# The softmax heads' product of probabilities and first values in three rounded products, in a two-block transformer forward on one Trainium2 core

## The reference

```python
s = jnp.einsum('bhid,bhjd->bhij', q, k) * scale     # 256 x 256 for each head
s = jnp.where(mask, s, -jnp.inf)
p = jax.nn.softmax(s, axis=-1)
o = jnp.einsum('bhij,bhjd->bhid', p, v)             # the product that is changed
```

## Time and profile before

| what | value |
|---|---|
| time of the profiled execution | 1799.72 us |
| its span | 1797.8 us |
| PE busy | 1788.5 us, 99% |
| DVE busy | 1243.6 us, 69% |
| ACT busy | 1037.5 us, 58% |
| POOL busy | 154.5 us, 9% |
| median of the timed runs | 1800.09 us |

### The profile page before, as it was taken

The page is one execution under the profiler, slowest core; times in us unless marked ns, Lnnn a source line. Parts: engine busy times, 40 slices in busy tenths (PEclk is TensorE's granted clock), DMA queues, the critical chain, the costliest instruction groups (busy, mean ns, idle before and its releaser), DMA issues.

```text
span 1797.8 us, 27226 instructions
## 1 busy us (share of the span) xinstructions
PE 1788.5 (99%) x10842; PEld 1622.1 (90%) x10842; DVE 1243.6 (69%) x1711; ACT 1037.5 (58%) x1638; POOL 154.5 (9%) x116
## 2 busy tenths in 40 slices
PE   9999999999999999999999999999999999999998
PEld 8999889888899999998889999898888999989987
DVE  6665656665666897687658888776565888767764
ACT  7435546774557765875554345576454444457853
POOL 0000000110011111100001211000000111100110
PEclk9999999999999999999999999999999999999999
DMA  9557555555555555445566655555555655555564
GB/s 370 200 171 225 182 182 190 181 175 195 190 189 167 171 171 175 154 165 169 194 207 202 199 188 176 193 180 172 190 193 196 201 199 181 174 192 183 168 220 140
DMA packets 95901, 340.30 MB, mean 189 GB/s; under 512 B 10800, under 2 KB 11184, under 8 KB 95648
## 3 DMA queue, kind: packets, MB, share of 16 engines
q1 hardware_dynamic: 94400, 334.44, 55.9%
q0 software_dynamic: 944, 3.61, 0.6%
q10 hardware_dynamic: 432, 0.53, 0.1%
HBM read 336.44 MB, written 2.10 MB: 188 GB/s over the span
## 4 chain that ended last, share of the span: by engine, by line
PE 99%; DMA 0%; DVE 0%; issue 0%; ACT 0%; DVEq 0%
PE ACC L838 15%; PE ACC L840 15%; PE ACC L839 15%; PE ACC L846 12%; PE ACC L843 12%; PE ACC L845 6%; PE ACC L844 6%; PE ACC L851 2%; PE ACC L852 2%; PE ACC L853 2%; PE PM L961 1%; PE PM L998 1%; PE PM L976 1%; PE PM L890 1%; PE PM L960 0%; PE PM L999 0%
## 5 line engine op out<-in xcount | busy, mean ns | idle before, releaser
L1654 DVE TENSOR_TENSOR WL<-RAW,WH 128x1024 fp32r<-128x1024 f32 (+2 forms) x631 | 793.4, 1272 | 421.8 <-ACT WH L1222 420.3
L1222 ACT ACTIVATE WH<-RAW 128x1024 fp32r<-128x1024 f32 (+2 forms) x632 | 646.9, 1038 | 382.5 <-PE ACC L840 190.2
L843 PE MATMUL ACC<-XHL,WH 128*128 128x512 f32 x1024 | 395.6, 386 | 0.0
L846 PE MATMUL ACC<-XHL,WH 128*128 128x512 f32 x1024 | 391.2, 382 | 0.0
L838 PE MATMUL ACC<-WH,XHL 128*128 128x512 f32 (+1 forms) x788 | 296.5, 376 | 0.0
L840 PE MATMUL ACC<-WH,XHL 128*128 128x512 f32 (+1 forms) x788 | 291.9, 370 | 0.0
L839 PE MATMUL ACC<-WL,XHL 128*128 128x512 f32 (+1 forms) x788 | 291.9, 370 | 0.0
L845 PE MATMUL ACC<-XHL,WL 128*128 128x256 f32 x1024 | 281.6, 275 | 0.0
L844 PE MATMUL ACC<-XHL,WL 128*128 128x256 f32 x1024 | 279.1, 273 | 0.0
L845 PEld LDWEIGHTS ACC<-XHL,WL 128*128 128x128 f32 x1024 | 193.5, 189 | 27.4
L844 PEld LDWEIGHTS ACC<-XHL,WL 128*128 128x128 f32 x1024 | 193.6, 189 | 26.5
(11 more groups left out here) (406 smaller groups left out, 2344.0 us busy)
## 6 DMA issues: line engine op xcount, KB each, us to landing
RAW<-in_w SPq DMA_DIRECT2D x607, 512.0 KB, 3.3
RAW<-in_wv SPq DMA_DIRECT2D x24, 344.0 KB, 3.2
X<-in_x SPq DMA_DIRECT2D x4, 512.0 KB, 11.9
Y<-in_xT SPq DMA_DIRECT2D x3, 512.0 KB, 10.6
out<-Y SPq DMA_DIRECT2D x6, 256.0 KB, 3.6
S<-in_bias POOLq DMA_DIRECT2D x8, 128.0 KB, 2.3
S<-in_od_gate_w POOLq DMA_DIRECT2D x1, 1024.0 KB, 7.1
S<-in_final_norm POOLq DMA_DIRECT2D x1, 1024.0 KB, 6.3
```

The costliest lines, as they stand in the source:

```text
L843: e.matmul(acc[0], wh0, pairs, start=f, stop=False, skip_group_check=True)
L846: m = e.matmul(acc[1], wh1, pairs, start=False, stop=l, skip_group_check=True)
L1222: e.activation(hi, src, ACT.Copy).then_inc(s_hi)
L1654: e.tensor_tensor(lo, src, hi.bitcast(F32), ALU.subtract).then_inc(s_lo)
```

## The change

For the 32 softmax heads with values of 128 features ("narrow"), the product with the first 128 keys is made of three products of rounded parts, as the projections are. `vh` and `vl` are the high part and the remainder of the head's first values; `PH` and `PL` are those of the first 256 columns of the turned probabilities. The product with the second 128 keys stays plain.

- ACT, step `value_split`, three slots before `pT` (seven before `pv`): copies the 128 columns of first values, rounded, to one of two slots. POOL, in the same slot: subtracts for the remainder.
- ACT, step `pT`: in place of one copy of 384 columns, one of the last 128 and one of the first 256, rounded, into the single buffer PH.
- DVE, new step `pl`, two slots after `pT` and two before `pv`: subtracts PH from the bank in PSUM for the remainder PL. The bank is held until then.
- PE, step `pv`: waits for `s_vl` and `s_pl`, then three fp32r products of 256 columns and the plain one as before.
- The new buffers lie where ZC lies, which only layer 1 uses.

```diff
-        ZC = sb("ZC", 1024)
+        with ExitStack() as first:
+            ZC = sb("ZC", 1024, F32, first)
+        PVH = sb("PVH", 1024, F32R)
...
+        PH, PL = PVH[:, 0:256], PVH[:, 256:512]
+        def value_slot(g):
+            at = 512 + 256 * (g % 2)
+            return PVH[:, at:at + 128], PVH[:, at + 128:at + 256]
...
                         put(slot + every * r + late, step, first + h + (4 if step[0] == "p" else 0), 1)
+                        if step == "pT":
+                            put(slot + every * r + late - 3, "value_split", first + h + 4)
+                            put(slot + every * r + late + 2, "pl", first + h + 4)
...
@@ tensor, pT @@
-                read_out[b] = (s_pts, TURN[g])
+                read_out[b] = (s_pl, nth_narrow(g)) if narrow(g) else (s_pts, TURN[g])
...
@@ tensor, pv @@
-                    e.matmul(o[:, 0:256], v[0], p[:, 0:256], start=True, stop=False, skip_group_check=True)
+                    vh, vl = value_slot(g)
+                    e.wait_ge(s_vl, nth_narrow(g))
+                    e.wait_ge(s_pl, nth_narrow(g))
+                    e.matmul(o[:, 0:256], vh, PH, start=True, stop=False, skip_group_check=True)
+                    e.matmul(o[:, 0:256], vl, PH, start=False, stop=False, skip_group_check=True)
+                    e.matmul(o[:, 0:256], vh, PL, start=False, stop=False, skip_group_check=True)
                     e.matmul(o[:, 128:256], v[1], p[:, 256:384], start=False, stop=True, skip_group_check=True).then_inc(s_pv)
...
@@ scalar @@
                 e.wait_ge(s_pt, TURN[g])
-                e.activation(pt_slot(g), PM[b][:, 0:384], ACT.Copy).then_inc(s_pts)
+                if not narrow(g):
+                    e.activation(pt_slot(g), PM[b][:, 0:384], ACT.Copy).then_inc(s_pts)
+                    return
+                if g > 4:
+                    e.wait_ge(s_pv, TURN[g] - 1)
+                e.activation(pt_slot(g)[:, 256:384], PM[b][:, 256:384], ACT.Copy).then_inc(s_pts)
+                e.activation(PH, PM[b][:, 0:256], ACT.Copy).then_inc(s_ph)
+            def value_split(g, _):
+                v, job = values_at(g)
+                n = nth_narrow(g)
+                e.wait_ge(s_evA, at_A(*job))
+                if n > 2:
+                    e.wait_ge(s_pv, TURN[g] - 2)
+                e.activation(value_slot(g)[0], v[0], ACT.Copy).then_inc(s_vh)
...
@@ vector @@
+            def probabilities_low(g, _):
+                b = PT_BANK[g]
+                e.wait_ge(s_ph, nth_narrow(g))
+                e.tensor_tensor(PL, PM[b][:, 0:256], PH.bitcast(F32), ALU.subtract).then_inc(s_pl)
...
@@ gpsimd @@
+            def value_split(g, _):
+                v, _ = values_at(g)
+                vh, vl = value_slot(g)
+                e.wait_ge(s_vh, nth_narrow(g))
+                e.tensor_tensor(vl, v[0], vh.bitcast(F32), ALU.subtract).then_inc(s_vl)
```

More of the change, by code:

```diff
@@ L409, in program, with values_at, narrow, nth_narrow @@
         TURN = list(accumulate(0 if g >= 4 and first_of_pair(g - 4) else 1 for g in range(44)))
+        def values_at(g):
+            layer, n, h = head_of(g - 4)
+            c = slice(128 * h, 128 * h + 128)
+            return [tok(3 * n + 2 if layer else 5)[:, t, c] for t in range(2)], (layer, f"v{n}" if layer else "va", h // 4)
+        def narrow(g):
+            return g >= 4 and not is_diff(g - 4)
+        def nth_narrow(g):
+            return g - 3 if g < 12 else g - 11
         def masked(a):
@@ L613, in program @@
                     FEW_BANK = got[0]
+        PT_BANK = {item: got for x in plan.values() for step, item, got in x if step == "pT"}
         def around(p):
@@ L647, in program @@
             sem(n) for n in ("s_dg", "s_pa", "s_pe", "s_pk", "s_pc", "s_pm", "s_zero", "s_am", "s_tri", "s_la"))
-        s_neg = sem("s_neg")
+        s_neg, s_ph, s_pl, s_vh, s_vl = (sem(n) for n in ("s_neg", "s_ph", "s_pl", "s_vh", "s_vl"))
         s_lx, s_lc, s_ly, s_ld, s_so, s_sd, s_sa, s_or, s_on, s_gd1 = (
@@ L987, in values_of @@
                     return [tok(2)[:, t, c] for t in range(2)], 256, (2, "v0", h // 4)
-                c = slice(128 * h, 128 * h + 128)
-                return [tok(3 * n + 2 if layer else 5)[:, t, c] for t in range(2)], 128, (layer, f"v{n}" if layer else "va", h // 4)
+                v, job = values_at(g)
+                return v, 128, job
             def pv(g, b):
@@ L1594, in scalar @@
             steps = {"seed": seed, "warm": warm, "xt": xt, "squares": squares, "root": root, "rms_a": rms_a, "gates1": gates1, "selectors": selectors, "decay_cols": decay_cols,
-                     "decay_rows": decay_rows, "cols": columns_step, "rows": rows, "decay": decay, "pT": pT,
+                     "decay_rows": decay_rows, "cols": columns_step, "rows": rows, "decay": decay, "pT": pT, "value_split": value_split,
                      "norm_qk": norm_qk, "qkT": qkT, "scores": scores, "normal": normal, "silu_z": silu_z, "yT": yT, "mix1": mix1, "pv": pv, "ty": ty, "copied": copied, "silu": silu, "decays1": decays1,
@@ L2136, in vector @@
                      "decay": decay, "mscores": mscores, "norm_qk": norm_qk, "scale_k": scale_k, "scores": scores, "mix1": mix1,
-                     "mix2": mix2, "rsum": rsum, "pv": pv,
+                     "mix2": mix2, "rsum": rsum, "pl": probabilities_low, "pv": pv,
                      "yT": yT, "ty": ty, "taps": taps,
@@ L2286, in gained @@
                     e.tensor_tensor(Y3[:, t, c], X3[:, t, c], S0[:, c], ALU.mult).then_inc(s_gn)
-            steps = {"norm_qk": norm_qk, "scale_k": scale_k, "scores": scores, "gate_z": gate_z, "cols": columns_step, "tri": tri, "gate_w": gate_w,
+            steps = {"norm_qk": norm_qk, "scale_k": scale_k, "scores": scores, "value_split": value_split, "gate_z": gate_z, "cols": columns_step, "tri": tri, "gate_w": gate_w,
                      "gate_lru": gate_lru, "gate_c": gate_c, "load_mask": load_mask, "load_gain": load_gain, "gained": gained}
```

## The result

| | median us | lowest to highest | runs |
|---|---|---|---|
| before | 1800.13 | 1799.44 to 1802.01 | 10 |
| changed | 1805.47 | 1803.59 to 1806.86 | 10 |

The changed kernel is slower: the ratio is 1.0025, with a 95% interval from 1.0017 to 1.0033. Its profiled execution took 1803.84 us (span 1801.9), 4.1 us more than that of before.

A forecast was written before the change was run, and what follows sets the result against it. PE, busy 99% of the span, was taken as the bound. Lateness 6.8 plus 0.5 less gain 2.5 gave +4.8 us on the profiled 1799.72, 1804.5; the median lies 0.37 higher, 1804.9 us; eight-in-ten range 1801.5 to 1808.3.

The forecast's parts named there:

- The wait for `pl`: PE's pv, heads 24 to 30: DVE lags 1.1 us a round, so PE waits from head 25, 6.1 us late at head 30.
- The products: PE's pv, 32 heads: three fp32r products in place of two passes save 0.095 us a head, 3.0 us over all.
- (a): `pl` on DVE between a pair's two splits: hidden beside POOL's addition, adds 0; if not, 0.42 us a round.
- (b): ACT's two `pT` copies instead of one: lengthen DVE's round by 0.08 us, 0.6 us in all (0 to 1.9).
- (c): ACT's `value_split`, behind one split and ahead of splits that DVE takes after 3.4 us of rotary work: adds 0.
- (d): POOL's subtraction directly behind its addition: a DVE split is already waiting, so 0; some 0.45 us a round if POOL goes first.
- Head 38: Heads 32 to 39, outside the stretch: PE waits 0.5 us for `pl`, between 0 and 1.3.
- A: Rival: `pl` is in time and only the matmuls' gain of 3.0 us is left, 1797.1 us; chance 0.08.
- B: Rival: DVE's rounds in the stretch stay at 12.67 us, 2.6 us less than forecast, 1802.3 us; chance 0.12.
- C: Rival: POOL's subtraction, or `pl` behind POOL, holds a split each round, 3.2 us more, 1808.1 us; chance 0.12.
- D: Rival: the three products are no shorter than the two passes, 2.5 us more, 1807.4 us; chance 0.03.

## Why the prediction was right

It forecast 1804.9 us, in a range from 1801.5 to 1808.3; 1805.47 came, and 1804.39 later. The first of these medians lies between two groups of executions, in a gap where no single one fell, so its nearness to 1804.9 says little; the steps say more:

- *The wait for `pl`, the term that decides.* Said: none at head 24, 0.5 us at head 25, about 1.2 at 26 to 29, near 2 at 30, from the lag of DVE's round. Measured: none, 0.68, 1.05, 1.80. The single waits differ because PE's rounds before were not 11.99 us each: five took 12.12 (the first two rows) and the last 11.37, where head 30 then waits more. The lag in sum is what was forecast: PE's pv of head 30 comes 78.54 us after that of head 24, where it was 71.96 before: 6.6 us more, against 6.8 said. Shown by the moved `pl` (waits gone, time below before) and by the plain heads. One thing the working left out: it said that the lag eats only the lead of the splits, and with `pl` out of the way it is first the rotary evacuation and `pl`, and then a split, that PE comes to wait for.
- *The products: mis-sized.* Said: 0.095 us a head, from steps of 0.112 us; measured: steps of 0.118, three of them 0.354 us in place of 0.43, so 0.076 a head (a round in layer 0 takes 12.36 us instead of 12.44). So the heads outside the stretch gave 1.9 to 2.0 us and not 2.5. The row that I took the step from the earlier trace rows reads its moving operand in another order; the kernel with parts in two halves shows that this is the difference.
- *(a), `pl` hidden beside POOL's addition: right.* The second split of the pair takes 1.96 us instead of 2.31, and the mask behind it starts 3.35 us after the pair's start (1525.71 to 1529.06), as before (3.37, 1501.49 to 1504.86). With `pl` behind the pair the round grew by 0.35.
- *(b), ACT's copies: right, 0.06 instead of 0.08.* The wait for ACT is 1.11 us instead of 1.05, and is 1.05 again with plain heads. The round grew from 13.11 to 13.16. ACT's rows for it, copies and splits of the values among them, in the changed kernel:

```profile
1532.82 0.26 ACT L1402 ACTIVATE SC<-PM 128x128 f32<-128x128 f32 x1
1532.98 0.37 ACT L1403 ACTIVATE PVH<-PM 128x256 fp32r<-128x256 f32 x1
1533.24 1.05 ACT L1254 ACTIVATE WH<-RAW 128x1024 fp32r<-128x1024 f32 x1
1534.19 0.30 ACT L1411 ACTIVATE PVH<-S 128x128 fp32r<-128x128 f32 x1
1534.39 2.00 ACT L1254 ACTIVATE WH<-RAW 128x1024 fp32r<-128x1024 f32 x2
```

- The two copies hold the split back for 0.42 us (1532.82 to 1533.24) where the one of 384 columns held it for 0.37. The values' copy stands behind that split, as (c) had it, and what the round grew by is already accounted for by (b).
- *(d), POOL's subtraction: right.* POOL in the changed kernel:

```profile
1525.87 2.19 POOL L2261 TENSOR_TENSOR S<-S 128x512 f32<-128x512 f32 x1 [9.57 <-DVE S L1775]
1528.02 1.44 POOL L2290 TENSOR_TENSOR PVH<-S,PVH 128x128 fp32r<-128x128 f32 x1
```

- It is issued right behind the addition, lasts 1.44 us where the shortest of its line lasts 0.45, and ends at 1529.46, 0.33 after the split (1529.13): it waited for the split, not the split for it. The Trainium skill's rule (SBUF — State Buffer, "Who interferes with whom"), that issue order decides who blocks, agrees with this trace.
- *Head 38.* Said 0.5 us (0 to 1.3), measured 0.24 (0.3 with the step behind a wait).
- *The sum.* Said +4.8 for the profiled execution: measured 6.6 + 0.3 - 1.9 = 5.0, less 0.8 for an idle time at one weight load (L853, layer 1; 0.7 us idle, 0.8 from matmul to matmul) that only the profile of before has: 4.2, where the two executions differ by 4.1. That 0.8 was not part of any step; with one profile of before it can't be told whether it is usual. So part of the nearness is luck: the products gave 0.6 us less than said, the waits were 0.4 shorter, and the 0.8 came from elsewhere.
- *The rivals.* A (no wait) fails on the rows of heads 25 to 30; its time, 1797.1, is 0.8 us below what the kernel with `pl` earlier in all heads reached, which has hardly a wait left. B (a round of 12.67) and C (POOL holds a split) fail on the round of 13.16 us and on POOL's row. D (products no shorter) fails on the round in layer 0, but it was a fifth of the way right: 0.02 of the 0.095 us was not there.

## What to carry to other kernels

Before an edit ties a bound engine to another one, take the round of both from the trace over several rounds: where the second is slower, its lag grows with every round, and the place within its round at which it delivers decides when the lead is gone. Here PE waited 6.7 us in six rounds for the same instruction at the late end of DVE's round, and 0.18 us with it in DVE's idle time some 6 us earlier, so look for the idle time first and put the new step there. Take an operation's price from a row that reads its operands in the same order, not only in the same size.

## What the runs showed of the hardware

- An fp32r product of 256 columns steps at 0.118 us with a dense moving operand and at 0.112 us with one whose columns are read in turn from two halves 128 columns apart.
- Writing the fp32r result in turn to two such halves makes a 128x256 copy from PSUM on ACT 0.62 us instead of 0.37, and a subtraction on DVE with one operand in PSUM, which then also reads its other operand in that order, 0.61 instead of 0.42.
- The first step behind a wait is longer: 0.192 to 0.195 us from L1028 to L1029 in the seven heads that waited, 0.115 to 0.126 in the other 25.
- A DVE operation with one operand in PSUM ran at its full speed of 0.42 us beside an addition on POOL that held up DVE's next split, with both operands in SBUF, for 0.74 us (1.96 against 1.22).
